# Second MLP: up projection of six of eight chunks by seven products of half blocks instead of eight, down weights staged by column halves, MLP loops written out

## The chip, the cores and the metric

The kernel runs on one core of a Trainium2 chip. The metric is the device time of one launch in microseconds (us), from the first to the last instruction with what lies around them. The engines named below are TensorE (PE, matrix products, with its weight loads as PEld), VectorE (DVE), ScalarE (ACT), GpSimd (POOL) and SyncE (SP, which issues the weight loads from HBM). Each has an instruction stream of its own, and they meet only at semaphores.

## The reference, cut to what matters

Two transformer blocks on a sequence of 1024 rows and a width of 1024, all in float32. The first has retention and gated linear attention as mixers and a squared-ReLU MLP, the second has three recurrent mixers, a cross attention and again an MLP. What the change touches is the MLP, which comes once in each block:

```python
def squared_relu_mlp(x, w1, w2):
    hdn = jnp.square(jax.nn.relu(jnp.einsum('bld,df->blf', x, w1.astype(jnp.float32))))
    return jnp.einsum('blf,fd->bld', hdn, w2.astype(jnp.float32))
...
    h = layer_norm(ALPHA * h + squared_relu_mlp(h, mlp_w1[l], mlp_w2[l]), ln3_g[l], ln3_b[l])
```

w1 is 1024 x 4096, w2 is 4096 x 1024.

## The kernel before, in words

**Products.** Every float32 operand of a large product is held as two float16 parts, a high part (the rounded value) and a low part (the rest). `gemm` (L678 to L687) makes each 128-deep step of a product by three matmuls, high by high (L684), high by low (L685), low by high (L686), each 128x128 weights against 128x512 columns.

**Chunks.** The 4096 hidden columns go in eight chunks of 512 (`NF`, `HALF`). For each chunk u the up projection is eight jobs (`hidden_job`: two sequence halves by four groups of 128 hidden columns, 8 deep, so 24 matmuls a job and 192 a chunk), and the down projection is sixteen jobs (`down_job`: eight row tiles by two column halves, 4 deep, 12 matmuls a job and again 192 a chunk). TensorE's order is up 0, up 1, down 0, up 2, down 1, ..., up 7, down 6, down 7.

**PSUM.** All these jobs use banks 0 to 3 in turn. `wide_bank` makes job j wait for `evac[j % 4]`, that the bank's previous job was taken out. For a down job it is VectorE that raises `evac` (`gated_add`, L2442: bank plus residual row in R). For an up job it is also VectorE, and not at once: ScalarE reads the bank and squares it into one of four buffers `TMP` (`hidden` in ScalarE's `mlp`, L1462 and L1741), and only VectorE's cast of that buffer into the high part of H (`split_piece`, L2084) raises `evac`; the low part follows (L2086).

```python
                dve.tensor_copy(hi, TMP[:, q % 4, :]).then_inc(evac[bank], 1)
                dve.drain()
                dve.tensor_tensor(lo, TMP[:, q % 4, :], hi, ALU.subtract).then_inc(piece_done, 1)
```

**Weights.** SP loads a chunk in two halves into the staging buffer WS (1 MB each), ScalarE rounds each half into the high part in WB and scales the rest (`round_half`, L1493 and L1495, 128x2048 each), and GpSimd subtracts to give the low part (`split`, L557). The subtraction also frees the half for the next load. WB has two slots, used in turn.

**VectorE's order in the MLP** is: the eight pieces of chunk u+1, then the sixteen `gated_add` of down u, and so on. **GpSimd's order** at the start of the second MLP is: the splits of up 0 and up 1, then `residual(2, "wo", 0)` (sixteen 128x1024 products and sums over R, L610 and L612), then the splits of down 0, up 2, and so on. In the first MLP, VectorE does setup work of another stage between the pieces (`s5_setup`, `s5_folds`, `s5_steps`), and GpSimd gates the last down weights (`gate_rows`).

Of the kernel before, what the change touches and what calls it, by code (L numbers as in the profile page):

```python
# [16 lines left out]
P = 128  # L17
SEQ = 1024
D = 1024
TT = SEQ // P  # L20
KT = D // P
HALF = 512
CHUNK = 64
EPS = 1e-5
# [94 lines left out]
def program(nc, I, out, block_decay):  # L119
    ctx = ExitStack()  # L120
    with ctx:
# [34 lines left out]
        w_split = sem("w_split")  # L156
        job_done = sem("job_done")
# [35 lines left out]
        NF = 4096 // HALF  # L193

# [4 lines left out]
        def deep(c):  # L199

            return WB[:, c % 2, :, :].rearrange("p l (k n) -> p l k n", k=4)
# [19 lines left out]
        N_ENGINES = 3  # L221

# [217 lines left out]
        def _(sp):  # L440
# [42 lines left out]
            def deep_chunk(c, src):  # L483

                for hf in range(2):
                    stage(c, hf, [(WS[:, hf, :].rearrange("p (k n) -> p k n", k=2),
                                   by_k(src)[:, 2 * hf:2 * hf + 2, :])])

            def mlp_stream(c0, w1, w2):
                wide_chunk(c0, [(w1, 0, HALF)])  # L490
                with sp.Fori(0, NF - 1) as j:
                    for hf in range(2):
                        sp.wait_ge(w_stage_free, 2 * (c0 + 1) + hf + 1 + 4 * j)
                        sp.dma_start(WS[:, hf, :].rearrange("p (k n) -> p k n", k=4),
                                     by_k(w1)[:, 4 * hf:4 * hf + 4, bass.ds((j + 1) * HALF, HALF)]
                                     ).then_inc(w_loaded[hf], 16)
                    for hf in range(2):
                        sp.wait_ge(w_stage_free, 2 * (c0 + 2) + hf + 1 + 4 * j)
                        sp.dma_start(WS[:, hf, :].rearrange("p (k n) -> p k n", k=2),
                                     by_k(w2)[:, bass.ds(4 * j + 2 * hf, 2), :]).then_inc(w_loaded[hf], 16)  # L500
                deep_chunk(c0 + 2 * NF - 1, w2[(NF - 1) * HALF:NF * HALF, :])

# [15 lines left out]
            mlp_stream(C["mlp1"], w_ff1, w_ff2)  # L518
# [15 lines left out]
            mlp_stream(C["mlp2"], w1_2, w2_2)  # L534
# [13 lines left out]
        def _(pool):  # L548
# [12 lines left out]

            def gate_columns(c, n):
# [9 lines left out]
            def gate_rows(c, i=0):  # L572

                row = S[:, 12, :].rearrange("p (a n) -> p a n", a=1).to_broadcast([P, 2, D])
                for hf in range(2):
                    pool.wait_ge(w_loaded[hf], loaded_at[c] + 32 * i)
                    w = WS[:, hf, :].rearrange("p (k n) -> p k n", k=2)
                    pool.tensor_tensor(w, w, row, ALU.mult)
                    pool.drain().then_inc(w_gated, 1)

            def split_narrow(c, width):
                n = 4 * width
                for hf in range(2):
                    pool.wait_ge(w_hi, 2 * c + 1 + hf)
# [31 lines left out]
            while c < N_CHUNKS:  # L616
                if c in (C["mlp1"], C["mlp2"]):
                    for u in range(2):
# [7 lines left out]
                    if gated:  # L626
                        split(c % 2, 2 * (c + 14) + 1)
                        need_wide(pool, LATE_JOBS[6])
                        need_wide(pool, LATE_JOBS[7])
                        gate_rows(c + 15)  # L630
                        split((c + 15) % 2, 2 * (c + 15) + 1)
# [6 lines left out]
                else:  # L638
                    split(c % 2, 2 * c + 1, 4)
# [15 lines left out]
        used_jobs = []  # L655


        @block.tensor
        def _(pe):
# [387 lines left out]
            def mlp(c0, src, last, rest_at):  # L1047
# [8 lines left out]
                def down_job(W, j, par):  # L1056
# [2004 lines left out]
```

## Time and profile before

| | us |
|---|---|
| median of three runs | 2814.84 (2813.55 to 2815.96) |
| span of the profiled execution, first to last instruction | 2814.4 |
| PE busy in it | 2653.3 (94%) |
| DVE busy | 1435.5 (51%) |
| ACT busy | 966.3 (34%) |
| POOL busy | 686.1 (24%) |

The times are those of the device, the rows those of one profiled execution. Its span is 0.4 us under the median of the runs, so a difference worked out in the span is carried to the median as it is. "Busy" of PE is from the start of a matmul to its modelled end; matmuls overlap, so their pace is read from their starts. A row of a timeline gives the start, the duration, the engine, the line, the operation, what it writes and reads, and in brackets the idle time before it with what ended it. The second MLP fills the last 670 us of the span.

### The profile page before, as it was taken

To read this page: it belongs to the slowest core of one execution; us is meant where nothing else is said; L and a number is where in the kernel's file an instruction comes from. 1 tells how busy PE (TensorE), PEld (TensorE's weight loads), DVE (VectorE), ACT (ScalarE), POOL (GpSimd) and SP (SyncE) were. 2 spreads that over 40 slices of the span, in tenths; PEclk is the share of its full clock that TensorE was granted. 3 is DMA by queue.
4 is the path that set the end of the run, shared out by engine and by line. 5 is a ranking of instruction groups with operands and counts; after the bars stand their busy time and mean duration, and the time that the engine had idled before them with its cause. 6 is when DMAs were issued, how large, how long until landed. Compare 5 with 4: busy or idle time off the path is not lost.

```text
span 2814.4 us, 33977 instructions
## 1 busy us (share of the span) xinstructions
PE 2653.3 (94%) x13340; PEld 1368.6 (49%) x13340; DVE 1435.5 (51%) x2294; ACT 966.3 (34%) x1154; POOL 686.1 (24%) x355
## 2 busy tenths in 40 slices
PE   6999999888999999999978899888999999999998
PEld 3677766444444444444454444344544444444443
DVE  6255344565744444675675749654336622222225
ACT  3434315035223332334244353253425332332231
POOL 1212024012212212321542231126013621221222
PEclk9999999999999999999989999999999999999999
DMA  7311131202111101221021230110001111110111
GB/s 302 117 60 68 43 120 46 90 30 90 54 37 60 60 30 60 75 96 40 31 90 66 70 116 30 45 44 32 31 30 60 60 42 49 60 60 31 60 45 60
DMA packets 55590, 182.44 MB, mean 65 GB/s; under 512 B 3952, under 2 KB 4368, under 8 KB 48016
## 3 DMA queue, kind: packets, MB, share of 16 engines
q1 hardware_dynamic: 47136, 138.89, 14.5%
q10 hardware_dynamic: 8304, 41.46, 4.0%
q8 instruction: 105, 1.72, 0.3%
q14 instruction: 45, 0.37, 0.0%
HBM read 170.90 MB, written 9.45 MB: 64 GB/s over the span
## 4 chain that ended last, share of the span: by engine, by line
PE 77%; DVE 9%; ACT 4%; POOLq 3%; DVEq 3%; issue 2%; POOL 1%; DMA 1%; ACTq 1%; SPq 0%
PE PS L684 23%; PE PS L685 23%; PE PS L686 23%; POOLq L613 1%; DVE XT L2086 1%; POOLq L611 1%; PE PS L723 1%; PE PS L1426 1%; POOL WB L557 1%; DVEq L2085 1%; PE PS L1399 1%; ACT WB L1493 1%; ACT WS L1495 1%; PE PS L972 1%; DMA Hf<-in_w_ada 1%
## 5 line engine op out<-in xcount | busy, mean ns | idle before, releaser
L557 POOL TENSOR_TENSOR WB<-WS,WB 128x512 f16<-128x512 f32 (+1 forms) x264 | 488.1, 1881 | 1854.4 <-ACT WS L1495 1854.1
L684 PE MATMUL PS<-XT,WB 128*128 128x512 f16 x1568 | 597.7, 381 | 10.5 <-DVE Hf L2084 5.3
L685 PE MATMUL PS<-XT,WB 128*128 128x512 f16 x1568 | 597.8, 381 | 0.0
L686 PE MATMUL PS<-XT,WB 128*128 128x512 f16 x1568 | 597.0, 381 | 0.0
L684 PE MATMUL PS<-WB,Hf 128*128 128x512 f16 x1440 | 551.5, 383 | 21.1 <-DVE Hf L2086 5.1
L685 PE MATMUL PS<-WB,Hf 128*128 128x512 f16 x1440 | 550.7, 382 | 0.0
L686 PE MATMUL PS<-WB,Hf 128*128 128x512 f16 x1440 | 550.3, 382 | 0.0
L2084 DVE CAST Hf<-S 128x512 f16<-128x512 f32 x172 | 148.8, 865 | 490.2 <-ACT S L1741 385.5
L1493 ACT ACTIVATE WB<-WS 128x2048 f16<-128x2048 f32 (+3 forms) x118 | 212.5, 1801 | 506.3 <-PE PS L686 471.1
L2442 DVE SCALAR_TENSOR_TENSOR R<-PS,R 128x512 f32<-128x512 f32 x208 | 143.0, 691 | 258.9 <-PE PS L686 251.8
L684 PEld LDWEIGHTS PS<-XT,WB 128*128 128x128 f16 x1568 | 154.2, 98 | 196.4 <-DVE XT L2086 5.5
L686 PEld LDWEIGHTS PS<-XT,WB 128*128 128x128 f16 x1568 | 154.1, 98 | 187.1 <-issue 3.8
L685 PEld LDWEIGHTS PS<-XT,WB 128*128 128x128 f16 x1568 | 154.0, 98 | 184.4 <-issue 3.1
L684 PEld LDWEIGHTS PS<-WB,Hf 128*128 128x128 f16 x1440 | 142.1, 99 | 198.6 <-issue 13.2
L686 PEld LDWEIGHTS PS<-WB,Hf 128*128 128x128 f16 x1440 | 142.0, 99 | 173.4 <-issue 6.3
L685 PEld LDWEIGHTS PS<-WB,Hf 128*128 128x128 f16 x1440 | 142.1, 99 | 172.8 <-issue 7.8
L1462 ACT ACTIVATE S<-PS 128x512 f32<-128x512 f32 x148 | 87.6, 594 | 393.5 <-PE PS L686 368.5
L1495 ACT ACTIVATE WS<-WS 128x2048 f32<-128x2048 f32 (+3 forms) x118 | 212.0, 1797 | 0.0
L684 PE MATMUL PS<-WB,XT 128*128 128x256 f16 (+2 forms) x640 | 169.0, 273 | 3.8 <-POOLq L588 2.3
L685 PE MATMUL PS<-WB,XT 128*128 128x256 f16 (+2 forms) x640 | 168.9, 273 | 0.0
L686 PE MATMUL PS<-WB,XT 128*128 128x256 f16 (+2 forms) x640 | 168.9, 273 | 0.0
L2086 DVE TENSOR_TENSOR Hf<-S,Hf 128x512 f16<-128x512 f32 x172 | 160.0, 930 | 16.2 <-issue 0.4
(381 smaller groups left out, 2744.2 us busy)
## 6 DMA issues: line engine op xcount, KB each, us to landing
WS<-in_w_ff SPq DMA_DIRECT2D x32, 1024.0 KB, 5.1
WS<-in_mlp_w SPq DMA_DIRECT2D x32, 1024.0 KB, 5.2
WS<-in_w_mix SPq DMA_DIRECT2D x20, 1024.0 KB, 4.9
Hf<-in_w_ada ACTq DMA_DIRECT2D x12, 1024.0 KB, 5.8
Hf<-in_w_ada SPq DMA_DIRECT2D x8, 1024.0 KB, 10.9
WS<-in_w_out SPq DMA_DIRECT2D x8, 1024.0 KB, 5.1
R<-in_x SPq DMA_DIRECT2D x4, 1024.0 KB, 9.9
R<-in_x ACTq DMA_DIRECT2D x2, 2048.0 KB, 7.9
```

The costliest lines, as they stand in the source:

```text
L557: op = pool.tensor_tensor(WB[:, slot, 1, at:at + n], WS[:, hf, i * n:(i + 1) * n], WB[:, slot, 0, at:at + n], ALU.subtract)
L611: pool.drain()
L613: pool.drain().then_inc(res_ready, 1)
L684: pe.matmul(o, ah, bh, start=(first and k == 0), stop=False, skip_group_check=True)
L685: pe.matmul(o, ah, bl, start=False, stop=False, skip_group_check=True)
L686: mm = pe.matmul(o, al, bh, start=False, stop=(last and k == n - 1), skip_group_check=True)
L1462: return act.activation(TMP[:, q % 4, :], src, func, scale=scale, bias=bias)
L1493: act.activation(rank_pair(hf, 0) if n == 64 else WB[:, slot, 0, hf * n:(hf + 1) * n], WS[:, hf, 0:n], ACT.Copy, scale=W_SCALE)
L1495: act.activation(WS[:, hf, 0:n], WS[:, hf, 0:n], ACT.Copy, scale=W_SCALE).then_inc(w_hi, 1)
L2084: dve.tensor_copy(hi, TMP[:, q % 4, :]).then_inc(evac[bank], 1)
L2086: dve.tensor_tensor(lo, TMP[:, q % 4, :], hi, ALU.subtract).then_inc(piece_done, 1)
L2442: dve.scalar_tensor_tensor(r, PS[:, b, :], 1 / (W_SCALE * scale * (ALPHA if first else 1.0)), r, ALU.mult, ALU.add).then_inc(evac[b], 1)
```

## The change

The diff leaves the arithmetic of the first MLP alone. In the second, chunks 2 to 7 (`FAST`) take another up projection. The chunk's 1024x512 weights are four blocks q11, q12, q21, q22 of 512x256, and the activations four blocks a11, a12, a21, a22 (row half by depth half). From them come sums, of the weights for each chunk (t1 = q12-q11, t2 = q22-t1, t3 = q11-t2, t4 = q21-t2) and of the activations once (s1 to s4). Seven products of such blocks, of 24 matmuls each, with sums of their results give the chunk that eight products gave before. They use PSUM banks 4 to 7. The parts of that:

- VectorE makes s1 to s4 once, in `corner_sums(j)`, called after each of the eight pieces of chunk 1 (eight instructions in each call).
- VectorE makes the four weight sums of a chunk, in place in WS (`form_sums`), between the `gated_add` of the down projection before; ScalarE rounds seven forms (`up_forms`, `last_form`), GpSimd subtracts seven (`split_forms`).
- ScalarE copies six partial results from PSUM into S (`keep`), VectorE adds them to later banks into TMP (`product_sum`), ScalarE squares in place, VectorE splits (`split_hidden`). The last product is issued after two down jobs.
- Down weights are loaded, rounded, split and waited for by column halves (`deep_chunk`, `split_down`, `need_half`), and down jobs run over eight row tiles for the first column half, then for the second, in both MLPs, except in the last chunk.
- The loops of both MLPs on SP, GpSimd, ScalarE and VectorE (`Fori`) are written out.

```diff
+        FAST = {"mlp1": range(0), "mlp2": range(2, NF)}
...
+        PRODUCTS = (("q21", "a12", 0), ("q11", "a11", 2), ("t1", "s1", 0), ("t2", "s2", 2), ("q22", "s4", 0),
+                    ("t3", "s3", 2), ("t4", "a22", 2))
...
@@ gpsimd @@
+            def split_down(m, u, gated=False):
+
+                c, slot = down_chunk(m, u), down_slot(m, u)
+                for hf in range(2):
+                    pool.wait_ge(w_hi, hi_count(c) + 1 + hf)
+                    n = slice(hf * 2048, (hf + 1) * 2048)
+                    pool.tensor_tensor(WB[:, slot, 1, n], WS[:, hf, :], WB[:, slot, 0, n],
+                                       ALU.subtract).then_inc(w_stage_free, 1)
+                    pool.drain().then_inc(w_half, 1)
+                pool.drain().then_inc(w_split, 1)
+
+            def split_forms(m, u):
+
+                at = FAST_BASE[m] + u - 2
+                for form in FORM_INDEX:
+                    pool.wait_ge(form_hi, 6 * at + FORM_HI[form])
+                    pool.tensor_tensor(form_at(m, u, form, 1), quad_stage(form), form_at(m, u, form, 0), ALU.subtract)
+                    pool.drain().then_inc(form_lo, 1)
+                    if form in ("t3", "t4"):
+                        pool.sem_inc(w_stage_free, 1)
...
                     for u in range(2):
-                        split((c + u) % 2, 2 * (c + u) + 1, 4)
-                    if c == C["mlp2"]:
+                        split((c + u) % 2, hi_count(c + u) + 1, 4)
+                    if m == "mlp2":
                         residual(2, "wo", 0)
-                    gated = c == C["mlp1"]
-                    with pool.Fori(0, NF - 1 - gated) as j:
-                        for u in range(2):
-                            split((c + u) % 2, 2 * (c + u) + 5 + 4 * j)
...
+                    for u in range(1, NF):
+                        if u in FAST[m]:
+                            split_forms(m, u)
+                        elif u > 1:
+                            split(up_chunk(m, u) % 2, hi_count(up_chunk(m, u)) + 1)
+                        split_down(m, u - 1)
...
@@ tensor @@
+                def fast_product(u, i):
...
+                    pe.wait_ge(form_lo, 7 * at + FORM_INDEX[form] + 1)
+                    for f in range(2):
...
+                        if form == "t1":
+                            pe.wait_ge(up_kept, 6 * at + 1 + f)
+                        if form == "t2":
+                            pe.wait_ge(up_sum, 6 * at + 1 + f)
...
+                for u in range(1, NF):
+
+                    c = up_chunk(m, u)
+                    if u in fast:
+                        if u == fast[0]:
...
+                            pe.wait_ge(corner_sum, 4 * (1 + (m == "mlp2" and len(FAST["mlp1"]) > 0)))
+                        for i in range(6):
+                            fast_product(u, i)
+                    else:
+                        pe.wait_ge(w_split, c + 1)
+                        for j in range(8):
+                            hidden_job(wide(c), j)
                     chunk_used()
-                    pe.wait_ge(w_split, c + 2)
-                    pe.wait_ge(piece_done, q0 + 8 * (u + 1))
+                    down_at[m, u - 1] = J[0]
+                    pe.wait_ge(piece_done, q0 + 8 * u)
                     for j in range(16):
-                        down_job(deep(c + 1), j, u % 2)
+                        if j % 8 == 0:
+                            need_half(u - 1, j // 8)
+                        down_job(u - 1, j % 8, j // 8)
+                        if j == 1 and u in fast:
+                            fast_product(u, 6)
...
@@ scalar @@
+                def up_forms(u):
...
+                    if u == fast[0]:
+                        act.wait_ge(job_done, used_jobs[up_chunk(m, u - 1)])
...
+                    for hf, forms in enumerate((("q11",), ("q21", "q22"))):
+                        act.wait_ge(w_loaded[hf], loaded_at[c])
+                        for form in forms:
+                            act.activation(form_at(m, u, form, 0), quad_stage(form), ACT.Copy, scale=W_SCALE)
+                        act.drain()
+                        act.activation(WS[:, hf, :], WS[:, hf, :], ACT.Copy, scale=W_SCALE).then_inc(form_hi, 1)
...
+                    for f in range(2):
+                        keep(0, f, f)
+                    squared(0)
+                    round_down(u - 1, 0)
+                    keep(1, 4, 0)
+                    squared(1)
+                    keep(1, 5, 1)
+                    for f in range(2):
+                        keep(0, 6 + f, f)
+                    round_down(u - 1, 1)
...
@@ vector @@
+                def corner_sums(j):
+
+                    k = j // 2
+                    a11, a12, x, y = kept(m, 0, 0), kept(m, 0, 1), kept(m, 1, 0), kept(m, 1, 1)
+
+                    def joined(dst, name):
+                        dve.tensor_tensor(dst, block_rows(name, 0, k), block_rows(name, 1, k), ALU.add)
+
+                    def parts(name, x):
+                        dve.drain()
+                        dve.tensor_copy(sum_rows(m, name, 0, k), x)
+                        dve.drain()
+                        return dve.tensor_tensor(sum_rows(m, name, 1, k), x, sum_rows(m, name, 0, k), ALU.subtract)
+
+                    if j % 2 == 0:
+                        joined(x, "a21")
+                        joined(y, "a22")
+                        joined(a11, "a11")
+                        joined(a12, "a12")
+                        dve.drain()
+                        dve.tensor_tensor(y, x, y, ALU.add)
+                        dve.tensor_tensor(x, a11, x, ALU.subtract)
+                        parts("s1", y)
+                    else:
+                        parts("s3", x)
+                        dve.drain()
+                        dve.tensor_tensor(y, y, a11, ALU.subtract)
+                        dve.drain()
+                        dve.tensor_tensor(a12, a12, y, ALU.subtract)
+                        parts("s2", y)
+                        parts("s4", a12)
+                        dve.drain().then_inc(corner_sum, 1)
...
+                    elif u == 1 and fast:
+                        hidden(u, corner_sums)
...
+                    def between(j):
+                        if u in fast and j in (1, 2):
+                            split_hidden(u, 5 + j)
+                        if u + 1 in fast:
+                            if j == 3:
+                                form_sums(u + 1, ("t1",))
+                            if j == 9:
+                                form_sums(u + 1, ("t2", "t3", "t4"))
```

## Rows read from the trace of the kernel before

**Rows 1.** Busy time by stretch; columns as in its header; second MLP's start, then its middle.

```profile
core 0: us, PE busy (x) PEld busy (x) DVE busy (x) ACT busy (x) POOL busy (x), PEclk, DMA share, GB/s
2186.00:2226.00 40.00, 36.17 (x164) 16.02 (x163) 36.78 (x16) 12.12 (x18) 35.81 (x14) 0.98 0.10 30
...
2352.00:2728.00 376.00, 376.00 (x1744) 170.46 (x1743) 105.49 (x145) 115.67 (x119) 73.04 (x18) 1.00 0.16 53
```

**Rows 2.** PE's timeline at full clock: two matmuls, 95 starts apart.

```profile
2054.84 0.39 PE L684 MATMUL PS<-WB,Hf 128*128 128x512 f16 x1 [1.93 <-DVE Hf L2086]
...
2075.35 0.38 PE L686 MATMUL PS<-WB,Hf 128*128 128x512 f16 x1
```

**Rows 3.** DVE's timeline, first MLP's first piece, and PE's next job.

```profile
649.77 0.43 DVE L2084 CAST Hf<-S 128x512 f16<-128x512 f32 x1
...
650.34 0.59 PE L684 MATMUL PS<-XT,WB 128*128 128x512 f16 x1 [5.26 <-DVE Hf L2084]
```

**Rows 4.** ACT's timeline, up 1 of the second MLP: its last job taken from PSUM.

```profile
2220.30 0.60 ACT L1462 ACTIVATE S<-PS 128x512 f32<-128x512 f32 x1 [3.88 <-PE PS L686]
```

**Rows 5.** DVE's timeline, the pieces of chunk 1 and the first and last add of down 0.

```profile
2188.49 0.43 DVE L2084 CAST Hf<-S 128x512 f16<-128x512 f32 x1 [4.61 <-ACT S L1741]
2189.01 2.69 DVE L2086 TENSOR_TENSOR Hf<-S,Hf 128x512 f16<-128x512 f32 x1
2191.61 2.56 DVE L2084 CAST Hf<-S 128x512 f16<-128x512 f32 x1
...
2212.76 2.57 DVE L2084 CAST Hf<-S 128x512 f16<-128x512 f32 x1
2215.42 4.55 DVE L2086 TENSOR_TENSOR Hf<-S,Hf 128x512 f16<-128x512 f32 x1
2219.89 4.28 DVE L2084 CAST Hf<-S 128x512 f16<-128x512 f32 x1
2224.26 0.69 DVE L2086 TENSOR_TENSOR Hf<-S,Hf 128x512 f16<-128x512 f32 x1
...
2228.50 0.69 DVE L2442 SCALAR_TENSOR_TENSOR R<-PS,R 128x512 f32<-128x512 f32 x1 [2.42 <-PE PS L686]
...
2267.35 0.69 DVE L2442 SCALAR_TENSOR_TENSOR R<-PS,R 128x512 f32<-128x512 f32 x1 [1.90 <-PE PS L686]
```

**Rows 6.** POOL's timeline, end of the residual and the splits of down 0.

```profile
2212.43 2.61 POOL L612 TENSOR_TENSOR R<-R,S 128x1024 f32<-128x1024 f32 x1
2215.35 8.54 POOL L557 TENSOR_TENSOR WB<-WS,WB 128x2048 f16<-128x2048 f32 x2 [0.31 <-issue]
...
2271.21 8.12 POOL L557 TENSOR_TENSOR WB<-WS,WB 128x2048 f16<-128x2048 f32 x2 [33.94 <-ACT WS L1495]
```

**Rows 7.** DVE's timeline in the first MLP, POOL busy from 719.57 to 728.28.

```profile
719.96 4.40 DVE L2086 TENSOR_TENSOR Hf<-S,Hf 128x512 f16<-128x512 f32 x1
724.44 0.69 DVE L2445 SCALAR_TENSOR_TENSOR S<-PS,S 128x512 f32<-128x512 f32 x1
725.23 3.60 DVE L2448 TENSOR_TENSOR R<-R,S 128x512 f32<-128x512 f32 x1
...
729.68 0.69 DVE L2448 TENSOR_TENSOR R<-R,S 128x512 f32<-128x512 f32 x1
730.45 0.69 DVE L2445 SCALAR_TENSOR_TENSOR S<-PS,S 128x512 f32<-128x512 f32 x1
```

**Rows 8.** PE's timeline and granted clock around the start of down 0.

```profile
2224.01 0.49 PE L684 MATMUL PS<-WB,Hf 128*128 128x512 f16 x1 [3.83 <-POOLq L560]
...
2227.65 0.38 PE L684 MATMUL PS<-WB,Hf 128*128 128x512 f16 x1
...
2224.00:2227.00 3.00, 2.99 (x8) 1.16 (x9) 1.89 (x4) 2.15 (x2) 0.00 (x0) 0.53 0.59 167
```

**Rows 9.** ACT groups of the second MLP by shape: count, busy us, mean ns.

```profile
L1493 ACT ACTIVATE WB<-WS 128x2048 f16<-128x2048 f32 x32 | 60.7, 1898 | 224.4 <-PE PS L686 220.3 <-DMA WS<-in_mlp_w 4.1
...
L1806 ACT ACTIVATE R<-R,SD 128x1024 f32<-128x1024 f32 x7 | 8.0, 1148 | 7.6 <-DVEq L2425 7.6
```

More of the change, by code:

```diff
@@ L1045, in _, with mlp @@
             pieces += 16
-            def mlp(c0, src, last, rest_at):
+            def mlp(m, src, last, rest_at):
+                c0, fast = C[m], FAST[m]
                 def hidden_job(W, j):
@@ L1726, in _, with mlp, hidden @@
                       second=False)
-            def mlp(c0, name, lnw, lnb, last):
-                def hidden(extra_j, extra_q, setup=None, first=False):
+            def mlp(m, name, lnw, lnb, last):
+                c0, fast = C[m], FAST[m]
+                def hidden(setup=None, first=False):
                     for i in range(8):
@@ L2482, in _, with mlp, hidden @@
             J[0] += 2 * TT
-            def mlp(gate, par, last):
-                def hidden(par_, extra_q, setup=None):
+            def mlp(m, gate, par, last):
+                fast = FAST[m]
+                def hidden(u, setup=None):
                     for j in range(8):
@@ new lines, in product_sum @@
+                def product_sum(u, n):
+                    at, f = FAST_BASE[m] + u - 2, n % 2
+                    bank, i, job, copy = ((4, 0, 2, 1), (4, 0, 8, 5), (6, 1, 10, 3))[n // 2]
+                    if n < 2:
+                        bank = 6
+                    dve.wait_ge(up_kept, 6 * at + copy + f)
+                    dve.wait_ge(up_done, 14 * at + job + f + 1)
+                    dve.drain()
+                    dve.tensor_tensor(TMP[:, (Q[0] + n - 2 * (n >= 2)) % 4, :], PS[:, bank + f, :], kept(m, i, f),
+                                      ALU.add).then_inc(up_sum, 1)
@@ new lines, in form_sums @@
+                def form_sums(u, forms):
+                    at = FAST_BASE[m] + u - 2
+                    for form in forms:
+                        if form == "t1":
+                            dve.wait_ge(form_hi, 6 * at + 1)
+                        else:
+                            dve.wait_ge(form_lo, 7 * at + 4)
+                        out, a, b = {"t1": ("q12", "q12", "q11"), "t2": ("q22", "q22", "t1"), "t3": ("q11", "t2", "q11"),
+                                     "t4": ("q21", "q21", "t2")}[form]
+                        dve.drain()
+                        dve.tensor_tensor(quad_stage(out), quad_stage(a), quad_stage(b),
+                                          ALU.subtract).then_inc(form_sum, 1)
@@ L2496, in down @@
+                def down(u, tail, between=None):
                     for j in range(16):
@@ L2524, in mlp @@
                     scale_rows(8).then_inc(ln_rows, 1)
[L2525 removed]
+                down(NF - 1, True)
                 if not last:
```

311 lines of the change are left out of this document (215 added, 96 removed).

## The prediction

> **What bounds the kernel now.** I read the busy time by stretch first. Over the middle of the second MLP PE is busy 376.00 of 376.00 us at full clock, DVE 105 us, ACT 116 us, POOL 73 us [rows 1]. There the pace of TensorE sets the time, and matmuls taken away are time taken away. In the 40 us in which up 1 runs it is another picture: DVE 36.78 us and POOL 35.81 us busy, PE with a gap [rows 1]. I then read the timelines of these three engines side by side, since the change puts its new VectorE work just there.
>
> **What TensorE saves.** Its pace is 95 starts in 20.51 us, 0.216 us a matmul [rows 2]. An up job of 24 matmuls is 5.18 us and a down job of 12 is 2.59 us. A product of half blocks is 24 matmuls too, seven in place of eight jobs: 5.18 us a chunk, and for six chunks **31.1 us saved**, if PE stays fed.
>
> **How TensorE is tied to VectorE.** In an up job `evac` is raised by VectorE's cast and not by ScalarE's read, so job j can't start before the cast of piece j-4. The trace shows the tie once: in the first MLP the fifth job waited 5.26 us and started at 650.34, 0.57 us after the first cast's start at 649.77 [rows 3]. So PE runs four jobs ahead of VectorE's casts at most, however many TMP buffers there are.
>
> **What VectorE has to do in up 1 now.** DVE takes the pieces of chunk 1 from 2188.49 on, PE's last job of up 1 is done at about 2220.2 [rows 4, 5]. The pieces take all this time because POOL works on `residual` and then the splits of down 0. Each cast or subtraction of VectorE, which takes 0.43 or 0.69 us alone, takes 2.56 to 2.70 us then. From 2191.61 to 2212.76 there are eight of them, 2.64 us each, one for each POOL instruction, and the two beside the 128x2048 splits take 4.55 and 4.28 us [rows 5, 6]. The first MLP shows for which kind of instruction it holds: beside POOL's work a float32 sum of two SBUF tensors took 3.60 us (alone 0.69), and the one before it that reads PSUM and SBUF kept its 0.69 us [rows 7]. Every instruction of `corner_sums` reads and writes SBUF, so I let it queue like these.
>
> A page has the rule. The Trainium skill, SBUF — State Buffer, section SBUF: two separate sides, says that a VectorE instruction with two SBUF inputs, or in a two-port mode, and a GpSimd instruction lock the shared pair of ports against each other for their whole length. The trace agrees for float32 inputs (4.40 and 3.60 us beside POOL); no row has a sum of two float16 inputs into float32 as `joined` is, and by the page it would wait too.
>
> **The cost of the corner sums, step by step.** The spacings without POOL: a cast and its drain 0.51 us (2188.49 to 2189.01) [rows 5], an SBUF two-input instruction of 512 with a drain behind it 0.77 us (729.68 to 730.45) [rows 7]; without a drain 0.61 us, since a cast starts 0.09 us before the end of the subtraction ahead of it (2191.61 against 2189.01 + 2.69) and the subtraction alone takes 0.69 [rows 5]. An even call is then 3 x 0.61 + 0.77 for the four joins, 0.61 + 0.77 for the two sums, 0.51 + 0.61 for the parts of s1: 5.10 us. An odd call is three casts at 0.51 and five at 0.77: 5.38 us. The piece before it is 1.12 us ahead of an even call and 1.28 us ahead of an odd one. Two pieces with their calls are 12.9 us, all eight 51.5 us, against 41.4 us of PE's up 1, and that without POOL.
>
> Now in order of time, on the rows of before:
> 1. Piece 0 as before, cast at 2188.49, subtraction to 2191.6 [rows 5].
> 2. The eight slots from 2191.61 that before took pieces 1 to 4 and more go to `corner_sums(0)`. The cast of piece 1 takes the slot of 2212.76, its subtraction that of 2215.42, the first cast of `corner_sums(1)` that of 2219.89. At 2224.26 POOL is idle [rows 5, 6].
> 3. The other seven instructions of `corner_sums(1)`: five at 0.77 and two at 0.51 us, 4.87 us, to 2229.1.
> 4. Pieces 2 to 7 with their calls: 3 x 12.88 = 38.6 us, to 2267.8.
> 5. Within step 4 PE ends up 1 (below), ACT rounds q11, q21 and q22 of chunk 2 (128x1024, under 1.15 us each, and two scalings of 1.9 us [rows 9]), and POOL subtracts q11 and q21, half of a 128x2048 split, 2.1 us each by 8.12 us for two [rows 6]. Each holds one VectorE instruction: +4.2 us, to 2272.0. The third form waits for VectorE's t1. Bounds: 0 if they fall into gaps, 4.2 as taken.
> 6. The first `gated_add` of down 0: 0.69 us and its drain, to **2272.8**.
>
> PE meanwhile: job 5 of up 1 (counted from 0) waits for the cast of piece 1 (end 2215.3, before it started at 2204.7), job 6 for piece 2's (2229.6), job 7 for piece 3's, down jobs 0 to 3 for those of pieces 4 to 7, and down job 4 for the first `gated_add`. So it has twelve down jobs left at 2272.8, 31.1 us. Before that it has idled some 4 us. Before, a gap of 3.83 us was followed by a granted clock of 0.53 (the 1.2 GHz level for most of it), and nine matmuls took 3.64 us (2224.01 to 2227.65) where 1.94 would be full pace: +1.7 us [rows 8]. I take the same once; the clock of the earlier gaps costs nothing, since VectorE is behind there. Bounds: 0 to twice that. Down 0 ends at 2272.8 + 31.1 + 1.7 = 2305.6.
>
> Before, it ended at about 2267.2, just ahead of the last `gated_add` at 2267.35 [rows 5]. **Lost: 38.4 us.** The 3.83 us gap of before and its slow clock lie inside this difference: down 0 by halves would have cured the gap (the first split is ready half of 8.54 us sooner [rows 6]), but VectorE holds PE then anyway.
>
> **The rest, in the steady chunks.** I followed one fast chunk from T, the start of its first product. PE is done with the products at T+5.2, 10.4, 15.5, 20.7, 25.9, 31.1, and with t4 at T+41.5. ACT (0.60 us a copy [rows 4], twice that with a square, 3.8 us a half of down weights by two of 1.9 [rows 9]) has the first copies at T+5.8 (wanted for t1 at 10.4), the second at T+14.8 and 16.7 (wanted from 20.7), the third at 18.7 and 21.3 (from 25.9); DVE has its sums at 8.5 and 11.1 (wanted for t2 at 15.5), 29.2 and 31.8 (for t4 at 36.3). Those of DVE read PSUM, which POOL does not hold up [rows 7]. POOL has the first half of the down weights at T+18.3 (wanted at 31.1), the second at T+33.8 (some 57). In the down projection the forms of the next chunk: ACT's first rounding after T+42.8, q21 and q22 by T+50, VectorE's t1 after the fourth add, the others after the tenth at T+63, t3 by T+68, all for products from T+77.7 on; t4 is rounded when the down projection is over and ready 3.2 us later, wanted 36 us later. The smallest slack is 4.6 us, and the extra work, some 15 us each of ACT, DVE and POOL a chunk, lies under PE, with engines half idle there [rows 1]. I price it at **0**. If one of these waits is late it costs its lateness six times.
>
> **Written out loops, column halves, the first MLP:** 0. PE waits for nothing there from 740 to 1260, the order of the roundings is the same, a half load is 1 MB as before, and the last down chunk keeps its order. If a wait for a half came late, four banks of down jobs, 10 us, would cover it.
>
> **Sum.** 2814.4 - 31.1 + 38.4 = 2821.7 in the span, **2822.1** at the median. What this kernel's measurement can tell from no change is about 0.2%, 5.6 us, so 2820.5 is the edge, and the forecast lies just over it.
>
> **The rivals.**
> A. *The corner sums don't queue behind POOL.* In step 2 the eight instructions take 5.1 us in place of 21.1; counted on, pieces 4 to 7 end at 2255.3 and the first add at 2256.1, 16.7 us sooner, with 5: 2805.4, faster. Against it: float32 instructions of both kinds are held [rows 5, 7]. If only the float16 joins went free, 8 us: 2814. By the Trainium skill, VectorE: DVE Perf Modes, section The perf-mode tier table, a tensor_tensor runs at twice the pace only at 16 bits; were the joins with their float32 output so fast, twelve of them outside POOL's time would save 0.27 us each, 3 us; I leave them at 1x.
> B. *PE runs ahead far enough*, because ACT empties the banks: the whole gain and the gap of before besides, 2814.8 - 31.1 - 5.5 = 2778. The code and [rows 3] speak against it.
> C. *A steady wait.* PE catches VectorE or ScalarE in each fast chunk, by the copies before t1 or the second ones before q22. It decides from 4.6 us of lateness on; at 5 us beyond that, six times, 30 us: 2852. For it speaks that a late first copy moves all behind it on ACT; against it that ACT has 116 of 376 us [rows 1] and no more than 32 of 77.7 then.
> D. *The change does not do what it says*, say PE's new jobs run at another pace. They have the same shape, 128x128 by 128x512; I give it little.
>
> **Chances.** Forecast 0.62, its own range 2811 to 2833 (0 to 4.2 in step 5, 0 to 3.4 for the clock, 5 us for the spacings of 80 instructions); A whole 0.10, A for the joins 0.10; B 0.04; C 0.12; D 0.02. The range reaches down to A and leaves out B, C and tails: 2803 to 2834. Slower by over 0.2%: C and 0.58 of the forecast, 0.48. Same: 0.37 of the forecast, the joins' case and D, 0.35. Faster: A, B and the forecast's low tail, 0.17.
>
> **What would show it.** In the changed kernel's timelines: DVE without a gap from 2188 to about 2272, eight instructions of 2.6 us after the first piece; PE's waits for the casts in up 1, from 3 to 9 us each; the end of down 0 some 38 us later than before; then PE at 0.216 us a matmul with no gap to the end, and fast chunks of 77.7 us a pair where there were 82.9. Wrong would be the prediction with corner sums of 0.6 us beside POOL's residual (A), no waits in up 1 (B), or repeated gaps from chunk 2 on (C).

## The result and the profile after

The changed kernel takes 2823.27 us (median of nine runs, 2822.11 to 2825.66) where the kernel before took 2815.91 us in the runs beside it (nine, 2813.55 to 2816.84): a ratio of 1.0027, 95% interval 1.0018 to 1.0037. It is slower by 7.4 us. The span of its profiled execution is 2822.0 us against 2814.4. The forecast was 2822.1 us, from a median of 2814.84 us for the kernel before: 7.3 us slower.

The busy time by stretch of the changed kernel; columns as in its header:

```profile
core 0: us, PE busy (x) PEld busy (x) DVE busy (x) ACT busy (x) POOL busy (x), PEclk, DMA share, GB/s
2186.00:2226.00 40.00, 26.15 (x113) 11.12 (x111) 36.43 (x15) 8.95 (x13) 36.71 (x14) 0.85 0.08 27
2226.00:2268.00 42.00, 27.90 (x95) 10.59 (x96) 38.60 (x61) 9.12 (x9) 4.79 (x2) 0.73 0.08 25
2268.00:2310.00 42.00, 37.40 (x168) 16.52 (x166) 21.21 (x26) 4.82 (x5) 11.41 (x5) 0.96 0.09 26
...
2352.00:2728.00 376.00, 376.00 (x1744) 170.46 (x1743) 165.54 (x196) 148.53 (x168) 118.55 (x45) 1.00 0.17 54
```

In the first stretch PE made 113 matmuls where it made 164 before [rows 1], at a mean granted clock of 0.85 (of full speed) and not 0.98. From 2352 on it is full again, 376.00 of 376.00 us, though DVE has 166 us there and not 105, ACT 149 and not 116, POOL 119 and not 73. So all of the loss lies before 2310, and the matmuls saved behind it pay most of it back.

The waits of PE in the changed kernel from 2100 us on, summed (who waited, for whom: us in total, times, longest):

```profile
PE PS L768 <- DVE Hf L2301: 28.0, 6, 9.2
PE PS L793 <- DVE XT L2301: 4.7, 7, 2.2
PE PS L768 <- DVE R L2659: 4.6, 1, 4.6
```

PE's timeline of the same kernel at the last of these waits (start, duration, engine, line, operation; in brackets the idle time before it and what ended it):

```profile
2273.08 0.61 PE L768 MATMUL PS<-WB,Hf 128*128 128x512 f16 x1 [4.60 <-DVE R L2659]
2273.49 0.63 PE L769 MATMUL PS<-WB,Hf 128*128 128x512 f16 x1
...
2275.94 0.38 PE L769 MATMUL PS<-WB,Hf 128*128 128x512 f16 x1
```

L2301 is the cast of `split_piece`, L2659 the `gated_add`. L793 is transpositions from 2112 to 2148 us, ahead of the second MLP; the kernel before waits 4.5 us there. What counts is six waits for casts of pieces, 28.0 us, and one for the first add of down 0, 4.6 us. The wait of before for the split of down 0 [rows 8] is gone. Behind the last wait seven steps from one matmul to the next take 2.86 us where 1.51 would be full pace; the granted clock is 0.53 from 2273 to 2276 (the 1.2 GHz level for most of it) and 1.00 behind it.

VectorE's timeline of the changed kernel from the first piece of chunk 1 to the adds of down 0 ("x4" is four merged instructions):

```profile
2188.92 0.43 DVE L2301 CAST Hf<-S 128x512 f16<-128x512 f32 x1 [4.61 <-ACT S L1870]
2189.44 2.68 DVE L2303 TENSOR_TENSOR Hf<-S,Hf 128x512 f16<-128x512 f32 x1
2192.04 8.94 DVE L2758 TENSOR_TENSOR S<-XT 128x512 f32<-128x512 f16 x4
2201.06 2.69 DVE L2772 TENSOR_TENSOR S<-S 128x512 f32<-128x512 f32 x1
...
2211.66 2.56 DVE L2301 CAST Hf<-S 128x512 f16<-128x512 f32 x1
...
2217.06 4.12 DVE L2762 CAST S<-S 128x512 f16<-128x512 f32 x1
2221.25 4.44 DVE L2764 TENSOR_TENSOR S<-S 128x512 f16<-128x512 f32 x1
...
2231.00 2.49 DVE L2758 TENSOR_TENSOR S<-XT 128x512 f32<-128x512 f16 x4
...
2247.78 2.19 DVE L2762 CAST S<-S 128x512 f16<-128x512 f32 x1
...
2251.95 2.17 DVE L2762 CAST S<-S 128x512 f16<-128x512 f32 x1
...
2272.34 3.04 DVE L2659 SCALAR_TENSOR_TENSOR R<-PS,R 128x512 f32<-128x512 f32 x4 [0.18 <-issue]
...
2305.71 0.69 DVE L2659 SCALAR_TENSOR_TENSOR R<-PS,R 128x512 f32<-128x512 f32 x1 [1.90 <-PE PS L770]
```

This is the answer to [rows 5]. The joins (L2758, the sums of two float16 blocks) take 8.94 us for four beside GpSimd's residual and 2.49 us for four when GpSimd is idle. The two casts of 2.19 and 2.17 us stand where GpSimd subtracts the first two forms (2247.43 and 2251.30); alone they take 0.43. The last add starts at 2305.71, 38.4 us later than the 2267.35 of before.

GpSimd's timeline of the changed kernel, the first half of the down weights in three fast chunks in a row:

```profile
2319.86 4.07 POOL L625 TENSOR_TENSOR WB<-WS,WB 128x2048 f16<-128x2048 f32 x1 [10.88 <-ACT WS L1621]
...
2397.56 4.07 POOL L625 TENSOR_TENSOR WB<-WS,WB 128x2048 f16<-128x2048 f32 x1 [10.89 <-ACT WS L1621]
...
2475.26 4.07 POOL L625 TENSOR_TENSOR WB<-WS,WB 128x2048 f16<-128x2048 f32 x1 [10.89 <-ACT WS L1621]
```

A pair of a fast up and a down projection repeats every 77.70 us, 7 + 8 times 5.18 us (a down projection is sixteen jobs of 2.59 us): nothing is lost in the steady chunks.

### The profile page after: what moved, and what is told of

Its sections match the earlier page's. It is cut to its first block, busy times and chain, and to the rows that moved or that the text cites. A ratio compares the mean times of both kernels' runs of the same rounds, so it can differ in the third digit from the quotient of the medians.

```text
span 2822.0 us, 33523 instructions
## 1 busy us (share of the span) xinstructions
PE 2630.9 (93%) x13196; PEld 1356.6 (48%) x13196; DVE 1550.9 (55%) x2418; ACT 1006.9 (36%) x1220; POOL 732.6 (26%) x385
## 4 chain that ended last, share of the span: by engine, by line
PE 77%; DVE 11%; ACT 4%; DVEq 3%; issue 2%; POOLq 1%; DMA 1%; ACTq 1%; POOL 0%; SPq 0%
PE PS L768 23%; PE PS L769 22%; PE PS L770 22%; DVE XT L2303 1%; PE PS L807 1%; PE PS L1552 1%; DVEq L2302 1%; ACT WB L1619 1%; DVE Hf L2303 1%; PE PS L1525 1%; ACT WS L1621 1%; PE PS L1056 1%; POOLq L693 1%; DMA Hf<-in_w_ada 1%; POOLq L691 1%
## 5 line engine op out<-in xcount | busy, mean ns | idle before, releaser
L614 POOL TENSOR_TENSOR WB<-WS,WB 128x512 f16<-128x512 f32 (+1 forms) x220 | 308.2, 1435 | 1220.8 <-ACT WS L1621 1220.8
L768 PE MATMUL PS<-XT,WB 128*128 128x512 f16 x1328 | 508.7, 383 | 28.8 <-DVE Hf L2301 23.5
L769 PE MATMUL PS<-XT,WB 128*128 128x512 f16 x1328 | 508.3, 383 | 0.0
L770 PE MATMUL PS<-XT,WB 128*128 128x512 f16 x1328 | 507.4, 382 | 0.0
L1619 ACT ACTIVATE WB<-WS 128x2048 f16<-128x2048 f32 (+3 forms) x106 | 189.8, 1791 | 333.4 <-PE PS L770 301.9
L2301 DVE CAST Hf<-S 128x512 f16<-128x512 f32 x124 | 97.8, 789 | 301.6 <-ACT S L1870 196.5
L2659 DVE SCALAR_TENSOR_TENSOR R<-PS,R 128x512 f32<-128x512 f32 x208 | 143.0, 691 | 194.4 <-PE PS L770 183.6
L625 POOL TENSOR_TENSOR WB<-WS,WB 128x2048 f16<-128x2048 f32 x32 | 131.2, 4099 | 374.3 <-ACT WS L1621 372.2
L768 PEld LDWEIGHTS PS<-XT,WB 128*128 128x128 f16 x1328 | 131.0, 99 | 188.0 <-DVE Hf L2301 19.2
L770 PEld LDWEIGHTS PS<-XT,WB 128*128 128x128 f16 x1328 | 131.1, 99 | 160.2 <-issue 6.1
L769 PEld LDWEIGHTS PS<-XT,WB 128*128 128x128 f16 x1328 | 130.9, 99 | 156.4 <-issue 4.3
L1621 ACT ACTIVATE WS<-WS 128x2048 f32<-128x2048 f32 (+3 forms) x106 | 189.2, 1785 | 0.0
L1588 ACT ACTIVATE S<-PS 128x512 f32<-128x512 f32 x112 | 66.2, 594 | 298.6 <-PE PS L770 273.6
```

The costliest lines, as they stand in the source:

```text
L614: op = pool.tensor_tensor(WB[:, slot, 1, at:at + n], WS[:, hf, i * n:(i + 1) * n], WB[:, slot, 0, at:at + n], ALU.subtract)
L625: pool.tensor_tensor(WB[:, slot, 1, n], WS[:, hf, :], WB[:, slot, 0, n], ALU.subtract).then_inc(w_stage_free, 1)
L768: pe.matmul(o, ah, bh, start=(first and k == 0), stop=False, skip_group_check=True)
L769: pe.matmul(o, ah, bl, start=False, stop=False, skip_group_check=True)
L770: mm = pe.matmul(o, al, bh, start=False, stop=(last and k == n - 1), skip_group_check=True)
L1588: return act.activation(TMP[:, q % 4, :], src, func, scale=scale, bias=bias)
```

## The experiments

The theory: the whole loss is VectorE's chain in chunk 1, the pieces and corner sums up to the first add of down 0. It has three parts, the sums' own work, its queueing behind GpSimd instruction by instruction, and a slow clock once. The rivals: the steady chunks cost something too; the first fast chunk is late because it waits for the sums; it is the release of the banks by VectorE that costs the time. All "us under" and "us over" are differences of medians. Each run was timed beside the kernel before on the same chip, which took 2817.81 us for the first four, 2816.16 for the next four and 2816.91 for the last three. The forecasts were made from 2815.9 and 2823.3, so what is compared is the distance to the kernel before.

**One part alone: the loops and the column halves.**

```diff
-        FAST = {"mlp1": range(0), "mlp2": range(2, NF)}
+        FAST = {"mlp1": range(0), "mlp2": range(0)}
```

> The changed kernel with the fast chunks empty in both MLPs, so only the written out loops and the down weights by column halves stay. Theory: the 3.83 us wait for the split of down 0 and the slow clock behind it go, 1.7 us: 2815.9 - 5.5 = 2810.4 us. Rival (PE then meets VectorE's casts or the second half at the same place, or the written out code costs something): 2814 to 2817.

Measured: 2812.23 us, 5.6 us under the kernel before, ratio 0.9981 (0.9971 to 0.9991). PE has no wait in the second MLP behind 2160 any more. In its VectorE timeline it is 73.2 us from the first piece of chunk 1 (2190.83) to the last add of down 0 (2264.07), where [rows 5] has 78.9: 5.6 us, the whole gain. So this part of the change gains by itself, by the gap at down 0 and the slow clock behind it, and the written out code costs nothing that shows.

**The sums left out.**

```diff
                 def corner_sums(j):
+                    if j % 2:
+                        dve.drain().then_inc(corner_sum, 1)
+                    return
...
-        PRODUCTS = (("q21", "a12", 0), ("q11", "a11", 2), ("t1", "s1", 0), ("t2", "s2", 2), ("q22", "s4", 0),
-                    ("t3", "s3", 2), ("t4", "a22", 2))
+        PRODUCTS = (("q21", "a12", 0), ("q11", "a11", 2), ("t1", "a21", 0), ("t2", "a22", 2), ("q22", "a21", 0),
+                    ("t3", "a11", 2), ("t4", "a22", 2))
```

> The changed kernel with the sums s1 to s4 of the activations left out: corner_sums only raises its semaphore, and the products that took s1 to s4 take plain blocks of the same shape. Theory (VectorE's chain in chunk 1 is the whole loss, the steady chunks cost nothing): 2815.9 - 31.1 for the matmuls - 5.5 for the gap and slow clock at down 0 that the column halves cure = 2779.3 us, no PE gap from up 1 on. Rival (copies, sums of products and forms hold PE in each fast chunk too): 2790 us or more, with gaps from chunk 2 on. Rival (the halves cure nothing): 2785.

Measured: 2781.54 us, 36.3 us under the kernel before where 36.6 was expected, ratio 0.9874 (0.9858 to 0.9891). No wait of PE is left behind 2160. So all else of the scheme, the forms, copies, sums of products and the late last product, holds PE nowhere, and the time fits that within the interval of some 5 us to either side. The rival of steady waits falls. Against the changed kernel's 7.4 us over, the sums cost 43.7 us where they stand: the 38.4 us of above and the cured gap that they hide.

**GpSimd's residual left out.**

```diff
                 for t in range(TT):
+                    if tail == 2:
+                        pool.drain().then_inc(res_ready, 1)
+                        continue
                     pool.tensor_tensor(R[:, t, :], R[:, t, :], S[:, rows_at, :], ALU.mult)
```

> The changed kernel without GpSimd's sixteen instructions of the residual ahead of down 0 in the second MLP (that scaling and shift of R is left out, the semaphores are raised). Theory (each SBUF instruction of VectorE waits for one of GpSimd): VectorE's pieces and sums of chunk 1 take about 52 us alone and 3 to 4 us beside each pair of splits or forms, so the first add of down 0 comes at about 2247.6 and not at 2272.3: 2798.6 us. Rival (the work of the sums alone decides, not GpSimd): 2820 to 2823.

Measured: 2801.54 us, 16.3 us under the kernel before (expected 17.3), ratio 0.9946 (0.9929 to 0.9964). Three lines of VectorE's timeline of this run, the cast of the first piece, the joins of the first call and the first adds of down 0:

```profile
2188.77 3.89 DVE L2304 CAST Hf<-S 128x512 f16<-128x512 f32 x1 [7.17 <-ACT S L1873]
...
2193.36 2.49 DVE L2761 TENSOR_TENSOR S<-XT 128x512 f32<-128x512 f16 x4
...
2247.56 3.04 DVE L2662 SCALAR_TENSOR_TENSOR R<-PS,R 128x512 f32<-128x512 f32 x4 [0.18 <-issue]
```

The four joins of the first call take 2.49 us and not 8.94, and the first add starts at 2247.56, 24.8 us sooner. Against the changed kernel's distance (7.4 us over) that is 23.7 us of the time. From the first piece to the first add it is 58.8 us here and 83.4 in the changed kernel, 24.6 us less, and the timelines tell it in two parts. 20.6 us are the eleven instructions from 2189.44 to 2214.30 that stood beside the residual, less their own time. 4.0 us come from the splits of down 0: in the changed kernel they hold two instructions of the chain (4.12 and 4.44 us at 2217.06 and 2221.25), here they run earlier, from 2184.04, and hold one, the first cast (3.89 us). So about 25 of the 38.4 us come with the residual, most of them VectorE's queueing behind it, and the rest stays although that is gone: 51 us of work against 41.

**Forms kept out of the sums.**

```diff
-                    pool.wait_ge(form_hi, 6 * at + FORM_HI[form])
+                    pool.wait_ge(form_hi, 6 * at + (max(FORM_HI[form], 3) if u == FAST[m][0] else FORM_HI[form]))
```

> The changed kernel, but in the first fast chunk GpSimd subtracts q11 and q21 only once t1 is rounded, so no form falls beside corner_sums. Theory: the two casts of 2.19 and 2.17 us are 0.43 us again, 3.5 us: 2819.8 us. Rival (the chain has room there): 2823.3.

Measured: 2820.47 us, 4.3 us over the kernel before, ratio 1.0015 (1.0006 to 1.0024), 3.1 us less than the changed kernel's 7.4 by two separate comparisons, whose intervals overlap; the step shows in the timeline. The first add of down 0 comes at 2268.63 and not 2272.34, from a first piece at 2188.77 and not 2188.92: 3.6 us. Two GpSimd instructions are worth as much as expected.

**Where the sums stand, and who waits for them.** Three kernels start the seven products one chunk later, at chunk 3, so they save 25.9 us of matmuls and not 31.1. They differ in the place of the sums.

```diff
-        FAST = {"mlp1": range(0), "mlp2": range(2, NF)}
+        FAST = {"mlp1": range(0), "mlp2": range(3, NF)}
...
-            return (C[m] + 1 + u) % 2
+            return (C[m] + u) % 2
...
+            if u == NF - 1 and u in FAST[m]:
+                return 1 - fast_slot(m, u)
```

and with the counts of chunks and pieces in the waits of the fast projection (`at` and what is made from it) one chunk later. In the first the sums stay in chunk 1:

> Seven products from chunk 3 on, corner_sums still all in the pieces of chunk 1. Theory (VectorE holds PE there through the banks, whoever wants the sums and when): one chunk's gain less, 5.2 us, and the two form subtractions of GpSimd no longer fall into the chain, 3.5 us: 2823.3 + 5.2 - 3.5 = 2825.0 us. Rival (PE is late because the first fast chunk waits for corner_sum): a whole chunk of room, about 2785 to 2790.

Measured: 2832.65 us, 16.5 us over the kernel before, ratio 1.0055 (1.004 to 1.007). The rival, that the first fast chunk waits for the sums, falls: with a whole chunk of room the time rose. But the size was missed, 9.1 us over the changed kernel's distance and not 1.7. GpSimd's timeline of this run, the two full splits of chunk 2 (merged, x2), and behind it VectorE's:

```profile
2248.81 8.53 POOL L616 TENSOR_TENSOR WB<-WS,WB 128x2048 f16<-128x2048 f32 x2 [22.92 <-ACT WS L1623]
```

```profile
2249.02 4.41 DVE L2766 TENSOR_TENSOR S<-S 128x512 f16<-128x512 f32 x1
2253.35 4.27 DVE L2303 CAST Hf<-S 128x512 f16<-128x512 f32 x1
```

I had counted the two form subtractions out and forgotten what takes their place: chunk 2 is an ordinary chunk now, so its two full splits of 128x2048 fall into the same chain and hold two instructions for 4.41 and 4.27 us, 7.6 us over their own time where the forms cost 3.5. That 4.1 us and the chunk's 5.2 make 9.3, where 9.1 was measured; from the first piece (2189.66) to the first add (2277.13) this run takes 87.5 us and not 83.4.

In the second the sums stand in chunk 2, after each piece:

```diff
-                    elif u == 1 and fast:
+                    elif u == 2 and fast:
                         hidden(u, corner_sums)
```

> Seven products from chunk 3 on, corner_sums all in the pieces of chunk 2, where GpSimd does no residual. Theory: VectorE starts its pieces some 12 us into up 2, needs 52 us for pieces and sums and 3.6 us beside two forms, 68 us in all where down 1's fifth job would start at 51.8: a stall of 16 us and 1.5 us of slow clock on 2784.5: 2802 us. Rival (without the residual the sums are hidden): 2784.5.

Measured: 2803.59 us, 12.6 us under the kernel before (expected 13.9), ratio 0.9952 (0.9937 to 0.9967). PE waits 10.0 us for casts and 4.2 us for the first add of down 1, 14.2 us where 16 was expected. The sums don't hide in one chunk even without the residual.

In the third they are spread:

```diff
-                    elif u == 1 and fast:
-                        hidden(u, corner_sums)
+                    elif u == 2 and fast:
+                        hidden(u, lambda j: corner_sums(3 + j // 2) if j % 2 else None)
...
+                        if last and u == 1 and j in (4, 8, 12):
+                            corner_sums(j // 4 - 1)
+                        if last and u == 2 and j == 5:
+                            corner_sums(7)
```

> Seven products for chunks 3 to 7 only (five chunks), and corner_sums spread: three calls between the adds of down 0, four between the pieces of chunk 2, one in down 1. Theory: with VectorE's idle time used nothing holds PE: 2815.9 - 25.9 - 5.5 = 2784.5 us, and no PE gap from up 1 to the end. Rival (the sums cost their time wherever they stand, since VectorE frees PE's banks): above 2800.

Measured: 2787.15 us, 30.7 us under the kernel before (expected 31.4), ratio 0.9891 (0.9874 to 0.9907). The same instructions cost nearly nothing where VectorE is idle. Its busy time by stretch, columns as in the first fence:

```profile
2226.00:2268.00 42.00, 42.00 (x197) 18.95 (x196) 30.94 (x43) 11.33 (x7) 8.83 (x4) 1.00 0.25 84
2268.00:2310.00 42.00, 42.00 (x196) 19.03 (x195) 28.48 (x44) 16.20 (x21) 8.20 (x3) 1.00 0.16 51
2310.00:2352.00 42.00, 40.38 (x188) 18.09 (x186) 31.33 (x33) 8.38 (x8) 16.25 (x7) 1.00 0.08 26
```

PE is full but for 1.6 us in the third stretch, a wait for one add of down 1, and VectorE busy 28 to 31 of 42 us in three stretches running, where [rows 1] has the engine at 105 of 376 us.

**Smaller GpSimd instructions.**

```diff
-                    pool.tensor_tensor(R[:, t, :], R[:, t, :], S[:, rows_at, :], ALU.mult)
+                    cols = [slice(0, D)] if tail != 2 else [slice(0, HALF), slice(HALF, D)]
+                    for n in cols:
+                        pool.tensor_tensor(R[:, t, n], R[:, t, n], S[:, rows_at, n], ALU.mult)
```

and the same for the addition.

> The changed kernel with each 128x1024 instruction of GpSimd's residual before down 0 as two of 128x512. Theory (one VectorE instruction is let through for each GpSimd instruction): about 18 and not 10 VectorE instructions pass from 2192 to 2218, eight at 0.65 us sooner, 5 us: 2818.5 us, and VectorE instructions of about 1.4 us there. Rival (the bytes that GpSimd moves decide): 2823.

Measured: 2823.38 us, 7.2 us over the kernel before, ratio 1.0026 (1.0017 to 1.0036): no gain. VectorE's timeline of this run:

```profile
2203.99 1.59 DVE L2306 TENSOR_TENSOR Hf<-S,Hf 128x512 f16<-128x512 f32 x1
...
2221.13 10.22 DVE L2761 TENSOR_TENSOR S<-XT 128x512 f32<-128x512 f16 x4
```

The mechanism shows, a VectorE instruction beside a half takes 1.6 us and not 2.7, and 22 instead of 13 instructions are through by 2221.2. But GpSimd pays as well: its residual takes 48.9 us (2171.81 to 2220.66 in its timeline) where it took 42.9. Part of that is the cutting itself. GpSimd's timeline of this run, two halves while VectorE is idle:

```profile
2183.48 2.50 POOL L692 TENSOR_TENSOR R<-R,S 128x512 f32<-128x512 f32 x2 [0.18 <-issue]
```

One whole takes 2.35 us (the median of 24 in the changed kernel), so the cut costs 0.15 us each, 2.4 us for sixteen by this estimate; the other 3.6 us would then go to the VectorE instructions, which are let in between twice as often. The two full splits hold two VectorE instructions' time in either kernel (here within four joins, 10.22 us where they take 2.49), but they are over 42.4 and not 36.2 us behind the first piece. From the first piece to the first add it is 83.0 us against 83.4. My forecast had left out what the halves and VectorE cost GpSimd.

**Who frees the banks.**

```diff
-                        to_tmp(PS[:, j % 4, :], ACT.Relu, scale=UNSCALE * F_SCALE ** 0.5)
+                        op = to_tmp(PS[:, j % 4, :], ACT.Relu, scale=UNSCALE * F_SCALE ** 0.5)
+                        if m == "mlp2":
+                            op.then_inc(evac[j % 4], 1)
```

and VectorE's cast no longer raises it there.

> The changed kernel, but in the second MLP ScalarE's read of an up job's bank raises evac, no longer VectorE's cast. Theory (the loss is VectorE's chain up to the first add of down 0, the bank rule only says where PE waits for it): the waits for the casts shrink or move to down 0, the first add stays near 2272, 2823.3 us, at most 1.5 less for a clock that stays up. Rival (it is the release of the banks by VectorE that costs the time): the 28 us of waits for the casts go, 2795.

Measured: 2824.0 us, 7.1 us over the kernel before, ratio 1.0028 (1.0018 to 1.0038). The waits of PE in the second MLP of this run (columns as above):

```profile
PE PS L768 <- DVE R L2663: 32.4, 1, 32.4
PE PS L768 <- ACT S L1588: 6.6, 2, 5.4
PE PS L768 <- issue: 0.5, 1, 0.5
```

Most of the waiting is in one place now, 32.4 of 39.5 us for the first add of down 0, and the time is the same. PE runs on through up 1 and four down jobs and then stands. ScalarE isn't free of VectorE either, since it writes into one of four buffers that VectorE must have read; its timeline of this run, the seventh piece:

```profile
2229.63 0.60 ACT L1588 ACTIVATE S<-PS 128x512 f32<-128x512 f32 x1 [12.80 <-DVE Hf L2307]
```

L2307 is the subtraction that reads such a buffer last. So the release of the banks decides where PE waits, and VectorE's chain decides how long.

**A version that beats both.** Two more on the spread kernel. `spread_frees` has the release of the banks by ScalarE as well:

> start3_spread with the same release by ScalarE. Theory: no wait for casts is left there, only 1.6 us for one add of down 1, which comes late behind the sixth call of corner_sums: 2785 to 2787 us, no change or 1 us less than start3_spread (30.7 us under the kernel before). Rival (VectorE's release still costs in every plain chunk): 5 us less.

Measured: 2786.16 us, 30.8 us under the kernel before, ratio 0.9891 (0.9874 to 0.9907), the 1.6 us wait still there. It is 0.1 us more of a gain than the spread kernel's, and the rival's 5 us don't show. `spread_early` moves four calls:

```diff
-                        hidden(u, lambda j: corner_sums(3 + j // 2) if j % 2 else None)
+                        hidden(u, lambda j: corner_sums({1: 3, 2: 4, 4: 5, 6: 6}[j]) if j in (1, 2, 4, 6) else None)
...
-                        if last and u == 2 and j == 5:
+                        if last and u == 2 and j == 12:
```

> start3_spread with the four calls in chunk 2 after its pieces 1, 2, 4 and 6 and the last call after the thirteenth add of down 1, so that none stands just before the adds of down 1. Theory: the last 1.6 us wait of PE in the MLP goes, 1.6 us less than start3_spread, about 32 us under the kernel before. Rival (the wait comes back at the pieces or at the start of chunk 3, for corner_sum): the same time or more.

Measured: 2784.91 us, 32.0 us under the kernel before, ratio 0.9881 (0.9865 to 0.9898). PE has no wait in it from 2160 to the end. The 1.3 us to the spread kernel are of the expected size, but the two intervals overlap, so that step alone is not shown by the times.

## Why the prediction was right, point by point

- **Time**: 2822.1 us forecast and 2823.27 measured, but as a difference 7.3 us and 7.4; of the 1.2 us between, 1.1 are the median of the kernel before, 2815.91 us in the nine runs and 2814.84 in the three that the forecast had.
- **Saving**: 31.1 us by 0.216 us a matmul. The steady pairs of 77.70 us are what it gave, and leaving the sums out brought 36.3 us with the cured gap of 5.6: 30.7 by measurement.
- **PE is tied to VectorE's casts**: six waits for them, 28.0 us. Two are in up 1, of 9.2 and 9.0 us, for the casts of pieces 1 and 2, as forecast for jobs 5 and 6; the forecast wait of job 7 did not come, and the four of the down jobs are 0.2, 5.1, 3.6 and 0.9 us. What PE waits there is VectorE's chain less its own work, so none of this changes the sum.
- **Steps 1 to 3**: piece 0's cast at 2188.92 (2188.49 before). `corner_sums(0)` took 19.6 us and not 21.1, since the four joins took 8.94 and not 10.6. The cast of piece 2 came at 2229.87, forecast 2229.1. The order of who held whom is not quite as written: the subtraction of piece 1 came early enough to stand beside the residual (2.66 us), and the two splits held the first cast and the first subtraction of `corner_sums(1)` (4.12 and 4.44 us), one instruction further on than forecast. The residual ended later than before, at 2216.4 and not 2215.0, and with it the splits, at 2225.1 and not 2223.9, which took back what the joins had given.
- **Step 4**: two pieces with calls took 12.84 us (from the cast at 2229.87 to that at 2242.71) where 12.88 was forecast from [rows 5, 7]; float16 joins have the pace of float32 sums, 2.49 us for four, some 0.61 us from start to start.
- **Step 5**: the two forms cost 3.5 us and not 4.2, and 3.6 us by the run that moved them. The forecast had added GpSimd's 2.1 us whole on top of the instruction's own time. But the casts start 0.35 and 0.65 us into GpSimd's instructions and are done 0.3 us behind their ends, 2.19 and 2.17 us with their own 0.43 in it.
- **Step 6**: the first add at 2272.34, forecast 2272.0, with 0.6 us in two pauses of VectorE before it ([0.18 <-issue] above and one of 0.42 at 2270.96) that the forecast had not. PE started again at 2273.08, forecast 2272.8.
- **Clock**: 1.35 us over seven steps, forecast 1.7. The granted clock of 0.73 from 2226 to 2268 cost nothing, as argued: with the banks freed by ScalarE the granted clock is 1.00 up to 2226 where it was 0.85, PE does its work earlier, and the time is the same.
- **Sum of the loss**: 38.4 us forecast and measured (2267.35 to 2305.71). That it fits to the tenth is luck: step 5 and the clock were high by 1 us together, steps 1 to 3 were low by 0.8 us (0.4 of it a first piece that came later), and the pauses of step 6 were left out.
- **The steady chunks at 0**: PE's 376.00 of 376.00 us, and no wait behind down 0. The working holds too: from T = 2305.51, the first matmul of chunk 2's products, ScalarE has its first copies at T+6.0 (forecast 5.8), VectorE its sums at T+8.8 and 11.4 (8.5 and 11.1), GpSimd the first half of the down weights at T+18.4 (18.3, 2319.86 + 4.07 in the fence above) and the second at T+34.0 (33.8).
- **The first MLP and the loops at 0**: the run of that part alone gained what the cured gap is worth and no more or less.
- **Rival A** fell by the joins (8.94 us for four beside GpSimd against 2.49) and by the run without the residual: the first add came sooner (24.8 us, where A had it 16.7 us sooner) only once GpSimd was idle. What the Trainium skill says in SBUF — State Buffer, section SBUF: two separate sides, of two SBUF inputs holds for float16 inputs too, which no row of before had shown: 8.94 us against 2.49. The Trainium skill's rule in VectorE: DVE Perf Modes, section The perf-mode tier table, that a tensor_tensor runs at twice the pace only at 16 bits, fits as well: with float16 inputs and a float32 output the joins kept the 0.61 us a step of float32 sums. No run here has a sum that is all 16 bits. **B** fell by the waits, **C** by the run without sums, **D** by the pace.

What I did not see lay not in this forecast but in those of two neighbours: that an ordinary chunk's splits would hit the chain harder than the forms (the run from chunk 3 with the sums left in place), and that halved instructions and VectorE slow GpSimd as well (the halves).

## What to carry to other kernels

Work saved on the bound engine is only worth what its feeder's one-time preparation leaves of it. Before such a change, lay the preparation out instruction by instruction on the timeline of the engine that does it, with what its neighbour does at that time, and find the stretches where both idle: here some 42 us of VectorE work cost 44 us of the time in one place (against the kernel without it) and about 1 us when spread over the 95 us from 2236 to 2331 in which VectorE had time to spare, and starting the seven products a chunk later (5.2 us given up) bought a gain of 32 us in place of a loss of 7. When a bank's release seems to hold an engine, ask what the releasing engine's queue ends in: moving the release moved the wait and not the time.

## What the runs showed of the hardware that I had not expected

- Where VectorE and GpSimd hold each other up, both pay. With GpSimd's instructions halved its own work grew from 42.9 to 48.9 us beside a busy VectorE, some 2.4 us of it for the cutting alone, which ate the gain.
- Beside 128x1024 instructions of GpSimd four joins in a row took 8.94 us and not four times 2.64. The trace of the changed kernel shows why, with the third and the fourth join asked for one by one and GpSimd's next instruction below them:

```profile
2197.56 2.83 DVE L2758 TENSOR_TENSOR S<-XT 128x512 f32<-128x512 f16 x1
2200.31 0.68 DVE L2758 TENSOR_TENSOR S<-XT 128x512 f32<-128x512 f16 x1
```

```profile
2200.31 2.89 POOL L690 TENSOR_TENSOR R<-R,S 128x1024 f32<-128x1024 f32 x1 [0.47 <-issue]
```

Three joins took 2.83 us each and the fourth its own 0.68 us. GpSimd had paused 0.47 us, two VectorE instructions went through one behind the other, and GpSimd's instruction took 2.89 us where the median is 2.35. So one for one is how two busy streams mostly went here, and not a rule without exception. Why GpSimd paused just there stays open.
